# A fused two-block layer stack on one Trainium2 core: the order of small products in the RWKV pairs, per-slab waits, and later side loads

## What is computed

```
for l in range(2):                                   # first block
    p = x @ w_in[l]                                  # u, q, k, v, zr, gates
    ys = [multiscale_pool(u), diff_attention(q, k, v), rwkv7_bidir(zr)]
    merged = sum_n sigmoid(gate_n + b_gate_n) * (ys_n @ w_branch[l, n])
    x = layer_norm(alpha * x + merged @ w_out[l])
    hid = relu(x @ w_up[l]) ** 2                     # 4096 wide
    x = layer_norm(alpha * x + hid @ w_down[l])
# second block, given c, c_ctx and 256 context rows ctx:
mod = silu(c) @ ada_w[i] + ada_b[i]                  # six rows per layer, also for c_ctx
layer 0: attention (RoPE, window of 128 and context keys, sinks) and SwiGLU, on x and ctx
layer 1: bidirectional state space mixer and SwiGLU; then a final RMS norm
```

## Time and profile before

| What | Value |
|---|---|
| Runs shown | 2546.51 us in the median of 3, 2545.81 to 2548.17 |
| The profiled execution | 2546.9 us |
| Its span, first to last instruction | 2545.1 us |
| Outside the span | 1.8 us |
| PE busy | 2476.9 us, 97% of the span |
| DVE, ACT, POOL busy | 1440.0 us, 524.4 us, 319.5 us |
| Granted TensorE clock, mean | 0.997 |

### The profile page before, as it was taken

How to read it: one execution, slowest core, us unless ns; L and a number is a source line. 1 busy time by engine, 2 the same in 40 slices (tenths; PEclk the granted TensorE clock), 3 DMA queues, 4 the chain that set the end, 5 groups by cost and what they waited for, 6 DMA issues and landing times. The chain is left out here.

```text
span 2545.1 us, 40375 instructions
## 1 busy us (share of the span) xinstructions
PE 2476.9 (97%) x16928; PEld 1891.9 (74%) x16928; DVE 1440.0 (57%) x2688; ACT 524.4 (21%) x1233; POOL 319.5 (13%) x367
## 2 busy tenths in 40 slices
PE   8999999999999999999999999999999999999998
PEld 7887786854788778685477747888886666666997
DVE  1576655855157665563357735555334488854775
ACT  1342220100134221010014910000003243411000
POOL 2002102210100220221000000000000155410110
PEclk9999999999999999999999999999999999999999
DMA  8332125887434112597631022322222534334553
GB/s 269 116 116 69 53 85 188 297 293 246 141 117 125 59 53 85 188 301 285 241 123 67 2 67 71 95 83 75 91 87 69 165 100 134 122 104 145 167 173 108
DMA packets 253611, 341.93 MB, mean 134 GB/s; under 512 B 7252, under 2 KB 179412, under 8 KB 253304
## 3 DMA queue, kind: packets, MB, share of 16 engines
q1 hardware_dynamic: 241632, 311.71, 37.6%
q10 hardware_dynamic: 8920, 17.67, 2.2%
q0 software_dynamic: 2880, 9.96, 1.1%
HBM read 338.13 MB, written 1.19 MB: 133 GB/s over the span
## 5 line engine op out<-in xcount | busy, mean ns | idle before, releaser
L1159 PE MATMUL PS<-MEM 128*128 128x256 f32 (+1 forms) x2632 | 447.9, 332 | 2.6 <-ACT MEM L1616 1.2
L1159 PEld LDWEIGHTS PS<-MEM 128*128 128x128 f32 x2632 | 406.3, 190 | 43.8 <-issue 1.9
L415 PE MATMUL PS<-MEM 128*128 128x256 f32 x1632 | 356.8, 379 | 1.1 <-DMA MEM<-w_up 1.1
L1575 ACT ACTIVATE MEM<-PS 128x256 f32<-128x256 f32 (+3 forms) x389 | 158.8, 439 | 923.7 <-PE PS L415 223.0
L415 PEld LDWEIGHTS PS<-MEM 128*128 128x128 f32 x1632 | 308.3, 190 | 44.7 <-DMA MEM<-w_up 2.3
L470 PE MATMUL PS<-MEM 128*128 128x512 f32 x608 | 265.3, 597 | 10.9 <-DMA MEM<-w_down 6.0
L2194 DVE SCALAR_TENSOR_TENSOR MEM<-MEM 128x512 f32<-128x512 f32 x280 | 216.4, 805 | 62.7 <-DMA MEM<-ada_w 57.2
L470 PEld LDWEIGHTS PS<-MEM 128*128 128x128 f32 x608 | 115.3, 191 | 156.9 <-issue 141.5
L3139 POOL TENSOR_TENSOR MEM<-MEM 128x1 f32<-128x1 f32 (+1 forms) x34 | 21.6, 636 | 1270.3 <-DVE MEM L2140 812.8
L704 PE MATMUL PS<-MEM 128*128 128x256 f32 x768 | 180.8, 386 | 0.0
L1472 PE MATMUL PS<-MEM 128*128 128x512 f32 (+1 forms) x512 | 171.6, 488 | 0.0
(11 more groups left out here) (400 smaller groups left out, 3283.6 us busy)
## 6 DMA issues: line engine op xcount, KB each, us to landing
MEM<-w_in SPq DMA_DIRECT2D x54, 1024.0 KB, 5.4
MEM<-ada_w SPq DMA_DIRECT2D x48, 1024.0 KB, 7.3
MEM<-w_up SPq DMA_DIRECT2D x32, 1024.0 KB, 5.6
MEM<-w_down SPq DMA_DIRECT2D x32, 1024.0 KB, 5.1
MEM<-ssm_w_in SPq DMA_DIRECT2D x24, 1024.0 KB, 5.5
MEM<-ffn_gate SPq DMA_DIRECT2D x22, 1024.0 KB, 5.3
MEM<-ffn_up SPq DMA_DIRECT2D x22, 1024.0 KB, 5.3
MEM<-ffn_down SPq DMA_DIRECT2D x20, 1024.0 KB, 5.1
```

Source lines behind the costliest of these rows:

```text
L415: ins = pe.matmul(bank[:, 0:T], W[:, k, c * P:(c + 1) * P], XT[:, k, :], start=k == 0, stop=k == KT - 1)
L1159: ins = pe.matmul(out, left[:, k, :], right[:, k, :], start=k == 0, stop=k == 3)
L1575: act.activation(out, view(b), func, **kw).then_inc(S("bank_read_by_act"), 1)
```

## The change

- `right_first` goes from level 3 to level 4, in front of the slot, and `right_second` goes directly behind that slot. Level 3 is left without both. ACT's copy of `rh` moves with them.
- `keys_flipped` of level 5 goes behind the slot, and its copy on ACT too.
- The slot `("z", 2)` gets one product in pairs 0 and 1; the slot "W" of pair 3 gets three in place of four. The slots then hold all 18 tiles, and `fill` behind the last pair issues nothing.
- The waits for `merged` and for all of `hid_squared` ahead of `wide` go. In the first half each slab waits for its own tiles.
- The load of `ctx` goes from POOL's queue to SP's, behind the fourth slab of `w_down` of layer 1, with a wait that all `up` products are done.
- ACT's five constant loads go behind its reads of the turned context tiles, in the middle of `w_down`.

```diff
-... ("z", 2): (0, 0, 3, 3), ...
+... ("z", 2): (1, 1, 3, 3), ...
-             "W": (3, 3, 3, 4), "XO": (2, 2, 2, 4), "sa": (2, 2, 2, 4)}
+             "W": (3, 3, 3, 3), "XO": (2, 2, 2, 4), "sa": (2, 2, 2, 4)}
@@ wide
                         W = b_slab(w, k0, 512 * half, n)
+                        if half == 0 and s == 3 and beside:
+                            beside()
+                        if half == 0 and ready:
+                            pe.wait_ge(S(ready[0]), ready[1] + k0 + n)
@@ pairs, PE
+                        if m == 4:
+                            right_first(gs)
+                        slot(pair, ("z", m))
+                        if m == 4:
+                            right_second(gs)
                         if m == LEVELS - 1:
                             for g in follow:
                                 keys_flipped(g)
-                        slot(pair, ("z", m))
-                        if m == 3:
-                            right_first(gs)
...
-                        if m == 3:
-                            right_second(gs)
@@ projections, PE
-                pe.wait_ge(S("merged"), l + 1)
-                wide(w_out[l], ..., by_token=True, turn=n0 + 1)
+                wide(w_out[l], ..., by_token=True, turn=n0 + 1, ready=("gated", 24 * l + 16))
...
-                pe.wait_ge(S("hid_squared"), (DFF // P) * (l + 1))
+                up_done = len(hist)
                 wide(w_down[l], ...
+                     ready=("hid_squared", DFF // P * l), beside=(lambda: ctx_at.append((len(slabs) - 1, up_done))) if l == DEPTH - 1 else None)
@@ pairs, ACT
+                        slot(("z", m))
                         if m == LEVELS - 1 and pair < 3:
                             flipped((2 * pair + 2, 2 * pair + 3))
-                        slot(("z", m))
-                        if m == 3:
+                        if m == 4:
                             for g in gs:
                                 copy(("rh", l, g), flat(RH[g % 2][:, :, :]), lambda b: b[:, 0:256], scale=-1.0)
@@ end of layer, ACT
                 if l == DEPTH - 1:
+                    squares2(0, (2, 3))
+                copy(("modrow", first), AROW, lambda b: b[:, 0:256])
+                if l == DEPTH - 1:
+                    act.wait_ge(S("x_gained"), NT * (2 * l + 2))
+                    modulated(0, (1,))
                     act.dma_start(ROT[:, :], io["rot"]).then_inc(S("const2_loaded"), 16)
                     ...
                     act.dma_start(DIAG[:, :, :], io["diag"]).then_inc(S("const2_loaded"), 16)
-                    squares2(0, (2, 3))
-                copy(("modrow", first), AROW, lambda b: b[:, 0:256])
-                if l == DEPTH - 1:
-                    act.wait_ge(S("x_gained"), NT * (2 * l + 2))
-                    modulated(0, (1,))
@@ POOL
-                    pool.dma_start(CTOK[:, :, :], io["ctx"]...).then_inc(S("ctx_loaded"), 16)
@@ SP
                 sp.dma_start(dst, src).then_inc(S(f"slab_loaded{s % NSLOT}"), 16)
+                if s == ctx_at[0][0]:
+                    sp.wait_ge(S("bank_filled"), ctx_at[0][1])
+                    sp.dma_start(CTOK[:, :, :], io["ctx"]...).then_inc(S("ctx_loaded"), 16)
```

More of the change, by code:

```diff
@@ L58 @@
 FILL_IN_PAIRS = 40 - FILL_LORA - FILL_DECAY - FILL_MEAN - FILL_VAR
-FILL_SLOT = {"mask": (4, 0, 0, 0), "begin": (12, 0, 0, 0), ("z", 1): (3,) * 4, ("z", 2): (0, 0, 3, 3), ("z", 3): (3,) * 4, ("z", 4): (3,) * 4, ("z", 5): (3,) * 4,
+FILL_SLOT = {"mask": (4, 0, 0, 0), "begin": (12, 0, 0, 0), ("z", 1): (3,) * 4, ("z", 2): (1, 1, 3, 3), ("z", 3): (3,) * 4, ("z", 4): (3,) * 4, ("z", 5): (3,) * 4,
              ("x", 1): (0,) * 4, ("x", 2): (0,) * 4, ("x", 3): (0,) * 4, ("x", 4): (0,) * 4, ("x", 5): (2,) * 4,
-             "W": (3, 3, 3, 4), "XO": (2, 2, 2, 4), "sa": (2, 2, 2, 4)}
+             "W": (3, 3, 3, 3), "XO": (2, 2, 2, 4), "sa": (2, 2, 2, 4)}
 V_MP, V_MN, V_W0, V_A0, V_KK, V_KA, V_RK, V_GG, V_GB, V_PS, V_BG, V_SG = 0, 15, 30, 38, 46, 50, 54, 58, 62, 66, 70, 94
@@ L349, in build @@
         NARROW_BANK = {"p1": 0, "p6": 1, "p7": 1, "p5": 2, "p4": 3, "p2": 4, "p3": 5}
-        narrow_at = []
+        narrow_at, ctx_at = [], []
         seven_at = []
@@ L438, in other_rows, with wide @@
                 pe.wait_ge(S("row_step"), row_steps[0])
-            def wide(w, src, nk, keyf, nt=NT, between=None, second=None, by_token=False, midway=None, turn=None):
+            def wide(w, src, nk, keyf, nt=NT, between=None, second=None, by_token=False, midway=None, turn=None, ready=None, beside=None):
                 for half in range(2):
@@ L1082, in _ @@
                     pass
-                pe.wait_ge(S("merged"), l + 1)
-                wide(w_out[l], lambda k, t: MRG[:, k, t * P:(t + 1) * P], KT, lambda h, t: ("wo", l, h, t), by_token=True, turn=n0 + 1)
+                wide(w_out[l], lambda k, t: MRG[:, k, t * P:(t + 1) * P], KT, lambda h, t: ("wo", l, h, t), by_token=True, turn=n0 + 1, ready=("gated", 24 * l + 16))
                 later = turn_banks(n0 + 1, 1)
@@ L1111, in _ @@
                     channels(w_up[l], 256 * s, 256, [("up", l, 2 * s), ("up", l, 2 * s + 1)], ("act", "act"))
-                pe.wait_ge(S("hid_squared"), (DFF // P) * (l + 1))
+                up_done = len(hist)
                 wide(w_down[l], lambda k, t: HID[:, k, t * P:(t + 1) * P], DFF // P, lambda h, t: ("dn", l, h, t), between=True, by_token=True,
-                     midway=(lambda: turn_normed(0, (1,))) if l == DEPTH - 1 else None, turn=n0 + 2 if l < DEPTH - 1 else None)
+                     midway=(lambda: turn_normed(0, (1,))) if l == DEPTH - 1 else None, turn=n0 + 2 if l < DEPTH - 1 else None,
+                     ready=("hid_squared", DFF // P * l), beside=(lambda: ctx_at.append((len(slabs) - 1, up_done))) if l == DEPTH - 1 else None)
                 ada_turned(ADA_DOWN + ADA_UP)
@@ L3192, in _ @@
                 else:
-                    pool.dma_start(CTOK[:, :, :], io["ctx"].rearrange("b (t p) d -> p (b t) d", p=P)).then_inc(S("ctx_loaded"), 16)
                     for t in RMS_TILES[0][:NT]:
@@ L3270, in _ @@
                 sp.dma_start(dst, src).then_inc(S(f"slab_loaded{s % NSLOT}"), 16)
+                if s == ctx_at[0][0]:
+                    sp.wait_ge(S("bank_filled"), ctx_at[0][1])
+                    sp.dma_start(CTOK[:, :, :], io["ctx"].rearrange("b (t p) d -> p (b t) d", p=P)).then_inc(S("ctx_loaded"), 16)
 def constants():
```

## The result

The changed kernel takes 2526.85 us (median of 4, 2525.68 to 2528.49), the kernel before 2546.5. The ratio is 0.9922, with a 95% interval from 0.9905 to 0.994: 19.7 us less, forecast were 19.0. The profiled execution has a span of 2525.6 us, 19.5 less than before.

A forecast was written before the change was run, and what follows sets the result against it. PE, busy 97% of the span, was taken as the bound, so only its idle stretches could change. Terms 5.4 + 3.6 + 0.3 + 2.1 + 0.3 + 7.3 = 19.0 us off 2546.5 gave 2527.5 us; 8-in-10 range 2523.5 to 2534.

The forecast's parts named there:

- two signs of being wrong: Waits at L826 behind level 3 in pairs 0 to 2, or a `w_down` wait over 1 us in layer 1.
- Right sides to level 4: Pairs, both layers: scores stop waiting for ACT to empty `rh`'s bank; less new waits in pair 3, 5.4 us gained.
- rival rotation: Pairs: the banks' rotation only moves, `rh` holds up other products as much, 5.4 us not gained, 2532.9; chance 0.08.
- `keys_flipped`, 3.6 us: Level 5 of the pairs: three filler products of 0.43 us cover the 0.7 us wait for DVE's mask; 3.6 us gained.
- Slot counts: Level 2 waits in pairs 0 and 1 go, 1.2 us; the wait behind the last pair grows, 0.9 back; net 0.3.
- Waits per slab at `w_out`: Start of `w_out`, both layers: first slab needs only finished tiles, so both waits of 1.03 us go; 2.1 us.
- Third slab, layer 0: Layer 0's `w_down`: of 2.15 us of waits gone, 0.3 counted, as PE then idles for the third slab; bounds 0 and 2.15.
- the half clock, given a quarter: Layer 0's `w_down`: idle of 2 us may bring a clock fall, plus 1.7 us, 2529.2; chance a quarter.
- Layer 1's `w_down`: First half: wait for squares 1.17, idle before third slab 4.41 and half clock 1.7 all go; 7.3 us.
- more than forecast: Rival: clock fall behind layer 1's pair 3 goes, 1.6 us, and layer 0's slab is early, 1.8; 2524, chance 0.06.
- the bytes come back: Rival: `ctx` on SP's queue delays `w_down`'s fifth slab, idle 2.3 us plus clock fall 1.7; 2531.5, chance 0.12.

The follow-up runs named there:

- e6_flipslots: Kernel before with only `keys_flipped` behind level 5's slot and the new slot counts (z2 of pairs 0 and 1, W of pair 3): 2540.3 us.
- e8_both: Changed kernel with POOL's gain rows and low-rank weights behind `w_down`'s first half, and two filler products kept for behind the last pair: 2521.88 us.
- e10_ctxpool: Changed kernel with the context rows back on POOL's queue at their old place, constants staying late: 2527.35 us.
- e11_again: The changed kernel run and profiled once more, nothing changed: 2525.57 us.
- e5_poolrows: Changed kernel with POOL's gain rows (both layers) and low-rank weights (layer 0) issued only when `w_down`'s first half is done: 2524.81 us.
- e3_loads: Kernel before with only the loads later: context rows behind `w_down`'s fourth slab on SP's queue, and the constants later: 2540.59 us.
- e1_rh: Kernel before with only both right sides moved to level 4, around its slot, ACT's copy of `rh` with them: 2537.15 us.
- e2_slabwaits: Kernel before with only the waits per slab for `w_out` and `w_down`: 2544.94 us.

## Why the prediction was right

It was right in the total (2527.5 against 2526.85) and in most steps. The two terms at `w_down` came out too small, and things that it had not counted made up for them. Of its own two signs of being wrong one came: a `w_down` wait over 1 us in layer 1 (1.40 us; the other, waits for DVE behind level 3 in pairs 0 to 2, did not).

- *Right sides to level 4, 5.4 us.* Right. The six waits were for the bank that ACT emptied, no rival rotation came, and pair 3 got its 0.6 us twice per layer. The edit alone showed 2.4 and, less clock and idle without a releaser, 2.7.
- *`keys_flipped`, 3.6 us.* Right: no wait of L819 for DVE is left, and `e6_flipslots` shows the same. The idle without a releaser that stands at L819 in layer 1 (1.65 us) is absent in `e8_both` and `e10_ctxpool`, where `keys_flipped` stands in the same place.
- *Slot counts, 0.3 us.* The wait at L1077 grew to 0.90, not 0.70, in each layer: 0.4 us less than that term. The product that stood ahead of the wait lasted 0.70 us with its tail (two records of L704 at 348.27 us, before), and the sum took 0.43 for it.
- *Waits per slab at `w_out`, 2.1 us.* Right, 2.6 in the stages.
- *Third slab, layer 0, 0.3 us.* The mechanism is right, PE idles 2.45 us (forecast about 2). The slab landed 16.2 us behind the end of `up`, as before (16.1): the earlier issue brought nothing, the lower bound of the term. And the half clock, given a quarter, came in this profile. The stage lost 3.57 us for the 1.7 gained ahead of it; in `e11_again`, without the half clock, the loss is 1.91. The rule of the Trainium skill's "DMA: Bandwidth & Descriptors", section "Queues, rings and completion order", on round-robin between queues was read as 0.7 us better; the landing doesn't show that. From 531 to 539 us, with work in both queues, POOL's moved 2.02 MB and SP's 1.00 MB, and the third slab, issued at 531.76, stood in SP's queue behind the ada slab.
- *Layer 1's `w_down`, 7.3 us.* Mis-sized: 1.17 and 4.74, 5.9 us. Counting 2.77 us for 1 MB and 2.2 fixed made the slab land at 13.3 us; it took 15.1, and PE idled 1.40 us where the prediction had none. SP's second and ada slabs and POOL's gain rows, 3 MB, were not all in before 12.4 us. The sum took the DMA engines as full once they had started, and they were not: for 2 us (the window below) they moved half of the 378 GB/s that it used, about 1.0 of the 1.8 us that it missed. Why, no run shows.

```profile
1158.00:1160.00 2.00, 2.00 (x6) 0.80 (x6) 0.00 (x0) 0.00 (x0) 0.00 (x0) 1.00 0.52 194
```

  `e5_poolrows` shows that the gain rows hold the slab up. The Trainium skill ("DMA: Bandwidth & Descriptors", section "Issuing engines are not separate DMA queues") has loads from all engines run on the same DMA engines and interleave; `e10_ctxpool` agrees with that, 2.3 us more idle for 1 MB more from POOL ahead of SP's slab. That the choice of queue is worth nothing, as the prediction took from it, was not tested.
- *Not counted.* Waits for `w_up` slabs (1.1 us before) are absent after, a half clock at 2250.7 too, 1.7 us, and one at 963.9 in layer 1's pairs, 1.7 us, which stood only in the rival "more than forecast"; without it the pairs gained 8.7 us, where the terms had 9.3. These made up for the terms that fell short. The first two can't be put down to the change: `e11_again`, the same kernel, has 0.9 us of such waits and a half clock at 2229.4. The agreement within 0.7 us is in part luck.

The rival "the bytes come back" didn't happen in the changed kernel, but did in `e3_loads`, `e5_poolrows` and `e8_both` (0.7 to 1.2 us at the fifth slab): what covered it, so far as the profiles tell, was the idle before the third (1.40 us there, and 1.00 in `e11_again`, which has none at the fifth either).

## What to carry to other kernels

Before taking a wait away, ask when the next input lands and what that landing is counted from. If full DMA engines set it, the earlier start turns into a longer idle stretch, and a long stretch can cost clock as well; move bytes out of the way first, and look again whether the wait is worth anything. Before a gain is put down to an edit, take a second profile of the same kernel: here half clocks of 1.7 us and waits of 1 us came and went between two. And a bank that the next products need should be emptied one group of products ahead: the copy was then free here.

## What had not been expected of the hardware

- Which idle stretch is followed by half clock is not fixed by its length. In the 13 profiles there are 18 stretches of 2.3 to 2.7 us in the second block (the place of the earlier trace rows) and before layer 0's third slab. Behind 7 of them the granted clock was 0.50 for 3.4 us, and in the two profiles of the changed kernel not behind the same one. The five of 3.7 to 6.2 us before layer 1's third slab were all followed by it: the 4.41 us of the earlier trace rows with 3.4 us, those of `e1_rh`, `e2_slabwaits`, `e6_flipslots` and `e10_ctxpool` with 6.8 us. These 6.8 us began while PE was still idle, so that PE was busy in 3.6 to 5.9 us of them, and half of that is the cost. Shorter idle stands ahead of a few others (0.93 and 0.79 us before 963.9).
- Idle of up to 1.65 us within runs of 64x64 products, with no releaser, came at the same instructions in both profiles of the changed kernel and at others in other kernels. In one layer's pairs it makes up to 3.5 us (`e2_slabwaits`), as much as an edit. It has a companion in the trace: a load of 16 KB of instructions. The first row is PE in the profile after, the second is from its DMA queues, 891.4 to 891.6 us.

```profile
893.98 0.56 PE L819 MATMUL PS<-MEM 64*64 64x64 f32 x11 [1.65 <-issue]
...
q8 instruction: 1, 0.02, 34.0%
```

  Between 190 and 1290 us the 13 profiles have 40 such stretches of 0.3 us or more, and every one ends 2.2 to 2.9 us behind the start of such a load, against 6 of 214 idle stretches with a named releaser. So PE seems to wait for its next instructions there. That is read from times alone; no run changed it.
